# A two-block language model layer on one core: RWKV's preparation cut by one halt more, and four smaller edits in the recurrent mixers

## The reference, cut to what matters

```
rwkv:  kk = l2norm(k * k_k);  k = k * (1 + (a - 1) * k_a)
       S_t = S_{t-1} * w_t + (S_{t-1} @ -kk) (kk * a)^T + v k^T;   y_t = S_t r_t
       y = layernorm(y) + sum(r * k * r_k) * v
mlstm: qk = silu(causal_conv(qk, 4 taps));  s = (q k^T) * exp(d - m), causal
       h = (s @ v) / max(|sum(s)|, exp(-m))
gdn:   decay_ts = exp(g_t - g_s), causal;   v and k scaled with beta
```

## Time and profile before

| | us |
|---|---|
| runs | 2463.22, 2467.28, 2469.05 |
| median | 2467.28 |
| profiled execution | 2466.33 |
| its span, first to last instruction | 2464.5 |
| TensorE busy | 2414.3 |
| VectorE busy | 1414.4 |
| ScalarE busy | 1130.9 |
| GpSimd busy | 111.8 |
| mean granted TensorE clock, of full | 0.995 |

### The profile page before, as it was taken

How to read it: one execution, slowest core, us unless ns; L and a number is a source line. 1 busy time by engine, 2 the same in 40 slices (tenths; PEclk the granted TensorE clock), 3 DMA queues, 4 the chain that set the end, 5 groups by cost and what they waited for, 6 DMA issues and landing times. The chain is left out here.

```text
span 2464.5 us, 34356 instructions
## 1 busy us (share of the span) xinstructions
PE 2414.3 (98%) x14480; PEld 2053.3 (83%) x14480; DVE 1414.4 (57%) x1836; ACT 1130.9 (46%) x1412; POOL 111.8 (5%) x100
## 2 busy tenths in 40 slices
PE   7999999999999999999999999999999999999998
PEld 7987989987888888888888878898888888888887
DVE  4766656677765555555555575444446545555554
ACT  6535435553454444444344464445544455444444
POOL 2100000220000000000000050000000000000000
PEclk9999999999999999999999999999999999999999
DMA  8633434654555566555555556655545544555564
GB/s 255 206 121 99 139 108 154 215 170 172 196 184 177 187 193 198 187 188 181 194 188 187 180 190 216 205 171 171 171 154 186 173 155 153 186 191 187 192 243 146
DMA packets 225641, 441.53 MB, mean 179 GB/s; under 512 B 11890, under 2 KB 28112, under 8 KB 223056
## 3 DMA queue, kind: packets, MB, share of 16 engines
q1 hardware_dynamic: 221744, 419.80, 51.8%
q0 software_dynamic: 3744, 19.53, 2.1%
HBM read 428.81 MB, written 10.49 MB: 178 GB/s over the span
## 5 line engine op out<-in xcount | busy, mean ns | idle before, releaser
L1268 ACT CAST ringH<-raw 128x1024 fp32r<-128x1024 f32 x780 | 817.1, 1050 | 1021.2 <-PE ps L602 877.7
L1866 DVE TENSOR_TENSOR ringL<-raw,ringH 128x1024 fp32r<-128x1024 f32 x780 | 952.9, 1238 | 451.1 <-ACT ringH L1268 450.1
L600 PE MATMUL ps<-ringH,nS 128*128 128x512 f32 x1376 | 553.9, 403 | 4.3 <-DVE ringL L1866 3.1
L602 PE MATMUL ps<-ringH,nS 128*128 128x512 f32 x1376 | 539.5, 392 | 0.0
L601 PE MATMUL ps<-ringL,nS 128*128 128x512 f32 x1376 | 538.9, 392 | 0.0
L628 PE MATMUL ps<-nS,ringH 128*128 128x256 f32 x1056 | 311.7, 295 | 9.1 <-DVE ringL L1866 7.5
L600 PEld LDWEIGHTS ps<-ringH,nS 128*128 128x128 f32 x1376 | 260.1, 189 | 59.7 <-DVE ringL L1866 6.5
L602 PEld LDWEIGHTS ps<-ringH,nS 128*128 128x128 f32 x1376 | 259.6, 189 | 55.8
L601 PEld LDWEIGHTS ps<-ringL,nS 128*128 128x128 f32 x1376 | 260.2, 189 | 49.8 <-issue 0.2
L629 PE MATMUL ps<-nS,ringH 128*128 128x256 f32 x1056 | 301.3, 285 | 0.0
L630 PE MATMUL ps<-nS,ringL 128*128 128x256 f32 x1056 | 301.1, 285 | 0.0
(11 more groups left out here) (414 smaller groups left out, 2132.4 us busy)
## 6 DMA issues: line engine op xcount, KB each, us to landing
raw<-in_w_in SPq DMA_DIRECT2D x189, 1024.0 KB, 5.1
raw<-in_ffn_w_gate SPq DMA_DIRECT2D x44, 1024.0 KB, 5.2
raw<-in_ffn_w_up SPq DMA_DIRECT2D x44, 1024.0 KB, 5.2
raw<-in_ffn_w_down SPq DMA_DIRECT2D x44, 1024.0 KB, 5.1
raw<-in_w_out SPq DMA_DIRECT2D x32, 1024.0 KB, 5.1
raw<-in_w_mem_kv SPq DMA_DIRECT2D x16, 1024.0 KB, 5.1
raw<-in_w_proj_a SPq DMA_DIRECT2D x8, 1024.0 KB, 5.2
raw<-in_w_proj_m SPq DMA_DIRECT2D x8, 1024.0 KB, 5.1
```

What stands on the lines that cost most here:

```text
L600: mm(o, XH[:, ts(j)], WH, first, False)
L602: t_of[0] = mm(o, XL[:, ts(j)], WH, False, last)
L1268: e.copy(ringH[:, h % NSPL, 0:nh * cols], raw[:, u % NRAW, h0 * cols:(h0 + nh) * cols]).then_inc(*hi.tick(h))
L1866: tt2(ringL[:, h % NSPL, o], raw[:, u % NRAW, h0 * cols:(h0 + nh) * cols], ringH[:, h % NSPL, o].bitcast(F32), SUB).then_inc(*lo.tick(h))
```

## The change

1. In RWKV's preparation the halt of `6 + 2 * hh` becomes two halts of `3 + hh`. TensorE's sums of squares and all behind them move behind the first one. ScalarE gets the new halt between the small projections' sigmoids and the exponentials, VectorE between the first difference of the decay and the rest.
2. For chunk 0 the copy of `NV` to `rhs` on VectorE is gone. TensorE reads `NV`, which ScalarE wrote, and waits for that and for the last level of the inverse.
3. ScalarE's square for the variance stands one halt earlier.
4. mLSTM's convolutions begin one halt later on all engines.
5. The mLSTM score tile has 384 columns in place of 512. The quarter that the causal mask makes zero is neither computed nor stored.
6. gdn's two broadcasts are made by transposing broadcast columns of `gcol` in place of multiplying `grow` rows with a column of the identity.

```
 TensorE, bcast
-  t = m1(b[:, 256 * j:256 * j + 256], ident[:, row + h + j:row + h + j + 1].broadcast_to([128, 128]), src, j == 0)
+  for tt in range(2):
+      t = e.transpose(b[:, 256 * j + 128 * tt:256 * j + 128 * tt + 128],
+                      gcol[:, tt, o + h + j:o + h + j + 1].broadcast_to([128, 128]), ident)
...
 TensorE, rwkv
   by_token(0, V_)
+  yield 3 + hh
   sums(rw_p, rw_a, (hh, "kk"), [u3(7)[:, k, :] for k in range(2)], 2)
-  yield 6 + 2 * hh
+  yield 3 + hh
...
-  e.wait_ge(*rw_v.at(hh, "rhs", c))
+  if c:
+      e.wait_ge(*rw_v.at(hh, "rhs", c))
+  else:
+      e.wait_ge(*rw_a.at(hh, "NV", 1))
+      e.wait_ge(*rw_v.at(hh, "inv", "xt", 4, 1))
   for n in range(4):
       inst = 2 * n + tt
-      t = m1(b[p, 64 * n:64 * n + 64], XR[p, inst, :], rhs[p, inst, :], n == 0)
+      t = m1(b[p, 64 * n:64 * n + 64], XR[p, inst, :], (rhs if c else NV)[p, inst, :], n == 0)
...
 TensorE, mlstm
-  for _ in range(4):
+  for _ in range(5):
       yield
...
-  t = m1(b[:, 256 * s:256 * s + 256], K[:, h, ts(s)], Q[:, h, :], s == 0)
+  t = m1(b[:, 256 * s:256 + 128 * s], K[:, h, ts(s)], Q[:, h, 128 * s:256], s == 0)
...
 ScalarE, rwkv
   ring.free(rw_a.now(), "rw", hh, "lora", q)
+  yield
   e.wait_ge(*rw_v.at(hh, "c"))
...
-  yield
   e.wait_ge(*rw_v.at(hh, "mu"))
   act(u3(0), u3(15), ACT.Square).then_inc(*rw_a.tick(hh, "var", 0))
+  yield
   square_roots(rw_v, rw_a, (hh, "var"), col_rw)
...
 ScalarE and VectorE, mlstm
   while not L.done(f"m{q}"):
       yield
+  yield
...
 VectorE, rwkv
   tt2(Wp, c_, sg, SUB).then_inc(*rw_v.tick(hh, "wp0"))
+  yield
   e.wait_ge(*rw_a.at(hh, "lo", 1))
...
-  if c == 0:
-      e.wait_ge(*rw_a.at(hh, "NV", 1))
-      e.tensor_copy(rv, nvv).then_inc(*rw_v.tick(hh, "rhs", 0))
-  else:
+  if c:
...
 VectorE, mlstm
-  tt2(S_, S_, ps3(ring.of("ml", "KQ", h), 2), MUL).then_inc(*ml_v.tick("S", h))
+  tt2(S_, S_, ring.of("ml", "KQ", h)[:, 0:384], MUL).then_inc(*ml_v.tick("S", h))
```

More of the change, by code:

```diff
@@ L715, in mem, with bcast @@
                 yield 2
-            def bcast(mk, name, src, row):
+            def bcast(mk, name, o):
                 for h in range(0, 4, 2):
@@ L721, in bcast @@
                     for j in range(2):
-                        t = m1(b[:, 256 * j:256 * j + 256], ident[:, row + h + j:row + h + j + 1].broadcast_to([128, 128]), src,
-                               j == 0)
+                        for tt in range(2):
+                            t = e.transpose(b[:, 256 * j + 128 * tt:256 * j + 128 * tt + 128],
+                                            gcol[:, tt, o + h + j:o + h + j + 1].broadcast_to([128, 128]), ident)
                     t.then_inc(*mk.tick(*name, h))
@@ L937, in rwkv @@
                     product("RB", Bt, Rt)
-                    rhs, Z = v3(SC + 512 * 13, 8, 64), v3(SC + 512 * 14, 8, 64)
+                    NV, rhs, Z = (v3(SC + 512 * k, 8, 64) for k in (6, 13, 14))
                     Sc = [v3(SC + 512 * 17 + 128 * k, 2, 64) for k in range(4)]
@@ L1012, in mlstm @@
                 for h in range(4):
-                    S_ = v3(MU + 1024 * (h % 2), 2, T)
+                    S_ = [v2(MU + 1024 * (h % 2) + 256 * s, 256 - 128 * s) for s in range(2)]
                     b = take("ml", "MB", h)
@@ L1033, in mlstm @@
                     for s in range(2):
-                        mm(b[:, 128 * s:256], mV[:, s, ts(h)], S_[:, s, 128 * s:256], s == 0, False)
+                        mm(b[:, 128 * s:256], mV[:, s, ts(h)], S_[s][:, :], s == 0, False)
                     for s, tt in ((0, 0), (0, 1), (1, 1)):
                         for c in range(2):
-                            o = 128 * tt + 64 * c
-                            t = m1(b[half(c), 256 + tt:257 + tt], S_[:, s, o:o + 64], ones[:, 0:1], False)
+                            o = 128 * (tt - s) + 64 * c
+                            t = m1(b[half(c), 256 + tt:257 + tt], S_[s][:, o:o + 64], ones[:, 0:1], False)
                     t.then_inc(*ml_p.tick("H", h))
@@ L1066, in gdn @@
                 e.wait_ge(*gt_v.at("end"))
-                bcast(gd_p, ("gb",), grows[2], 0)
-                bcast(gd_p, ("bb",), grows[1], 32)
+                bcast(gd_p, ("gb",), 0)
+                bcast(gd_p, ("bb",), 4)
                 yield 5
@@ L1608, in mlstm @@
                 for h in range(4):
-                    S_ = v3(MU + 1024 * (h % 2), 2, T)
+                    S_ = v2(MU + 1024 * (h % 2), 384)
                     e.wait_ge(*ml_p.at("MB", h))
@@ L2367, in mlstm @@
                     for s in range(2):
-                        t = tsc(S_[:, s, :], Mb, gcol[:, s, 8 + h:9 + h], 0.0, SUB, MAX)
+                        t = tsc(S_[:, 256 * s:256 + 128 * s], Mb[:, 128 * s:256], gcol[:, s, 8 + h:9 + h], 0.0, SUB, MAX)
                     t.then_inc(*ml_v.tick("s0", h))
                     e.wait_ge(*ml_a.at("S", h))
-                    tt2(S_[:, 0, 0:128], S_[:, 0, 0:128], mask(C_SI), MUL)
-                    tt2(S_[:, 1, 128:256], S_[:, 1, 128:256], mask(C_SI), MUL).then_inc(*ml_v.tick())
+                    tt2(S_[:, 0:128], S_[:, 0:128], mask(C_SI), MUL)
+                    tt2(S_[:, 256:384], S_[:, 256:384], mask(C_SI), MUL).then_inc(*ml_v.tick())
                     own(ml_v)
                     e.wait_ge(*ml_p.at("KQ", h))
-                    tt2(S_, S_, ps3(ring.of("ml", "KQ", h), 2), MUL).then_inc(*ml_v.tick("S", h))
+                    tt2(S_, S_, ring.of("ml", "KQ", h)[:, 0:384], MUL).then_inc(*ml_v.tick("S", h))
                     ring.free(ml_v.now(), "ml", "KQ", h)
```

## The result

The changed kernel takes **2449.59 us** (four runs, 2449.44 to 2452.89), beside 2468.16 us of the kernel before on the same chip (four runs, 2463.22 to 2469.22). The ratio is 0.9932, with a 95% interval of [0.9915, 0.9949]. It is faster, by 18.6 us or 0.7% by these medians; forecast were 2454.0 and a range of 2447 to 2463. The profiled execution took 2449.46 us with a span of 2447.7, which is 16.8 less than before.

A forecast was written before the change was run, and what follows sets the result against it. TensorE, busy 98% of the span, was taken as the bound: only its instructions, idle gaps or clock could save time. Terms summed to -13.3 us, giving 2453.0; with 0.95 for the median, 2454.0, range 2447 to 2463.

The forecast's parts named there:

- m1: mLSTM's second convolution group: gap of 3.85 goes, new gap of 1.9, 0.8 at ScalarE's copy; -1.8 us with clock.
- square: ScalarE's variance square a halt earlier: gaps 0.44 and 1.29 go, and the half-clock stretch from 387.1; -3.0 us.
- first preparation: RWKV's first half of heads: gap of 1.46 goes, TensorE waits 3.6 in the memory's factor; +2.1 us net.
- broadcast: gdn's broadcast: sixteen transposes replace eight matmuls of 256 on TensorE; -1.4 us.
- second preparation: RWKV's second half of heads: casts and subtractions go on, so the gap of 1.70 at 242.80 goes; -1.7 us.
- m0: mLSTM's first convolution group, a halt later: waits of 3.84 become 0.6, at the third piece; -3.2 us.
- copy: RWKV's first chunk read in place: the wait of 1.66 before its product goes in both halves; -3.3 us.
- Rival B: Memory's reciprocal not late, VectorE's subtractions 1 us quicker, no half clock follows in RWKV; -19.5 us, 2447.8; chance 0.10.
- the prediction's sign: On TensorE's timeline, the count of half-clock stretches before 400 us is two or less.
- A: Waits only move: mLSTM's convolutions and RWKV's second half of heads bring nothing; -6.6 us, 2460.7; chance 0.23.
- C: Transposes drop the clock behind gdn's broadcast: one half-clock stretch, +1.3 us, 2455.3; chance 0.05.
- D: Slower: eight convolution pieces before RWKV's chunk chain hold up TensorE, 21.8 us instead of 7.7; +5.8, 2473; chance 0.06.

The follow-up runs named there:

- e1: Changed kernel with the one further halt of RWKV's preparation taken out again on all three engines; 2449.34 us, ratio 0.9935.
- e2: Changed kernel with mLSTM's convolutions back at their old halt; 2453.30 us, ratio 0.9949.
- e3: Changed kernel with VectorE's copy of NV to rhs for chunk 0 put back; 2456.03 us, ratio 0.9955.
- e4: Changed kernel with ScalarE's square for the variance back at its old halt; 2455.22 us, ratio 0.9962.
- e5: Changed kernel with the mLSTM score tile at 512 columns again; 2449.80 us, ratio 0.9937.
- e12: Changed kernel with both the full mLSTM score tile and gdn's broadcasts as matmuls again; 2449.55 us, ratio 0.9939.
- e6: Changed kernel with gdn's broadcasts as matmuls again; 2449.76 us, ratio 0.9936.
- e8: Changed kernel with the memory stage one halt later, as in e7, and mLSTM's second convolution one halt later still; 2443.30 us, ratio 0.9908.
- e9: Changed kernel run once more with nothing edited; 2451.47 us, ratio 0.9946.
- e7: Changed kernel with one halt more in the memory stage, ahead of its mean; 2445.15 us, ratio 0.9919.
- e10: As e7, with mLSTM's second group of convolutions three halts later; 2444.49 us, ratio 0.9914.
- e11: As e10, with VectorE's four multiplications of gdn's keys by their decay moved behind the products; 2442.96 us, ratio 0.9909.

## Why the prediction was right

**The sum without the clock.** The forecast's terms hold -1.95 us of clock (-1.3 + 1.3 in the first half, -0.65 at m1, -1.3 at the square) and -11.35 of gaps and work. Span times clock fell by 11.7 (2451.35 to 2439.63). The whole agrees better than its terms, and that is luck: the first preparation cost 1.2 less than forecast and the broadcast gained 1.4 less, and the two cancel.

| part | forecast without clock | found, and how |
|---|---|---|
| first preparation | +2.1 | +0.9 in gaps, +0.6 to +1.0 by position (e1) |
| second preparation | -1.7 | -2.0 by position (e1) |
| mLSTM, m0 and m1 | -3.2 and -1.15 | -4.0 in gaps, -4.5 by span times clock (e2) |
| copy | -3.3 | -3.3 in gaps, -2.7 (e3) |
| square | -1.7 | -1.7 in gaps, -1.7 (e4) |
| score | -1.0 | -1.1 by position, -1.1 to -1.2 by span times clock (e5, e12) |
| gdn's broadcast | -1.4 | 0 (e6) |

The gaps and positions found add up to about -11.2, beside the 11.7.

*First preparation.* The step is right (the gap in `factor`, released by VectorE's reciprocal), its size was not. TensorE got there at 118.5, as counted (118.6). VectorE was 1.4 us earlier than counted, 120.8 in place of 122.2. VectorE's timeline after:

```profile
106.46 0.68 DVE L1908 COPY AR<-ps 128x512 f32<-128x512 f32 x1
...
110.61 0.20 DVE L2170 RECIPROCAL small<-small 128x8 f32<-128x8 f32 x1 [0.28 <-ACT small L1496]
110.73 2.31 DVE L1874 TENSOR_TENSOR ringL<-raw,ringH 128x1024 fp32r<-128x1024 f32 x2
112.95 0.16 DVE L2002 TENSOR_SCALAR small<-small 128x2 f32<-128x2 f32 x1
...
118.40 2.35 DVE L1874 TENSOR_TENSOR ringL<-raw,ringH 128x1024 fp32r<-128x1024 f32 x2
120.67 0.16 DVE L2005 RECIPROCAL small<-small 128x2 f32<-128x2 f32 x1
```

The first reciprocal was 0.6 later than counted (done at 110.8, not 110.2), though the root was waited for 0.28 and not 1.3, because the drain's copy (106.46) now stood ahead of it and VectorE's scaling beside GpSimd took 1.55 us where 0.62 was counted (105.50 before, 107.06 after). Behind it the memory's mean came at 112.95 where 114.2 was counted: the two subtractions took 2.31 us where I had kept the 3.36 of the earlier trace rows, although GpSimd was no longer beside them, and the copy that I had counted there was done. The long part behind it, 5.4, and the last two subtractions, 2.3, were as counted. Both errors were carried over from rows whose surroundings the change moves. Rival B had named the first, the subtractions.

*m1.* I forecast a gap of 1.9 and 3.07 came. GpSimd's and VectorE's timelines after, to the earlier trace rows:

```profile
195.37 3.25 POOL L2746 TENSOR_TENSOR AR<-AR 128x1024 f32<-128x1024 f32 x1 [33.73 <-ACT AR L1335]
```

```profile
195.36 1.22 DVE L1874 TENSOR_TENSOR ringL<-raw,ringH 128x1024 fp32r<-128x1024 f32 x1
199.20 1.53 DVE L2348 SCALAR_TENSOR_TENSOR AR<-AR,prm 128x256 f32<-128x256 f32 x3 [2.62 <-ACT AR L1587]
200.76 0.50 DVE L2295 TENSOR_TENSOR AR<-ps,AR 64x128 f32<-64x128 f32 x2
```

The scaling took 3.25 us, not 2.17, and VectorE's subtraction now starts with it (195.36), so the first piece came 1.1 us later. The pair stands side by side in all twelve executions that have mLSTM's later halt (3.25 or 3.26 us); in e2 and in the kernel before VectorE idles there, and it is 2.17. The rest is the forecast's mechanism: the piece in front of the addition. The 0.8 behind it, at ScalarE's copy, did not appear in the changed kernel; with the piece a halt later (e8) it does, as 1.09.

*m0.* Forecast 0.6 at the third piece, measured 0.32, from a masking as forecast. So m0 gave 3.5 in gaps (3.84 less 0.32) and m1 0.8 (3.85 less 3.07).

*Broadcast.* This step of the forecast failed: -1.4 was forecast and nothing came. I costed the removed work as time won because it stood on TensorE, without asking what TensorE would be waiting for next. The 1.43 at 502.80 in the trace of before, a low half on VectorE, was outside the stretch I had listed; on it the 1.4 had to be set off.

**The clock.** Forecast: the stretch at 103.8 goes and one comes behind `factor`, the one at 206.2 half goes, 387.1 goes. Profiled: seven became four, in the repetition five; up to 400 us three became two, in the repetition three. The stretch behind the gap of 2.37 us came in three of the eight kernels that have that gap (e3, e4, e9); the one behind the gap of 3.07 in seven of nine (not in e3, and in e7 it began before the gap had ended). So 1.3 as a certainty behind `factor` was too much. The price itself holds: a stretch costs 1.1 to 1.6 where it can be read. Which stretches come in one execution is chance, so that the profiled execution had two before 400 us, as the prediction's sign wanted, is luck; the repetition had three. The other signs came: no gap before the first chunk's product, before the square's sums or at the low half near 240. Those in `factor` and before the last chunk's product are there, at 2.37 and 3.07 where 3 to 4 and about 2 were named.

Mean spans say 2463.67 (27 runs of before) and 2449.43 (nine of the changed kernel): 14.2 less, against 13.3 forecast. Of the 14.2, 11.7 is work and gaps and 2.5 clock, by span times clock. The 18.6 of the first medians is more than the change is worth on average. The time forecast, 2454.0, started from a median of three runs, 2467.28, where the median of the 27 is 2465.09.

**The rivals.** A (the waits only move, 2460.7) is out: e2 shows mLSTM's part worth 4 us, and e1 the second preparation 2.0. It holds for one edit that it did not name, the broadcast. B (more than counted, 2447.8) is out: its reason was right (the subtractions were 1 us quicker), but the reciprocal was still late by 2.37 of the 3.6, and half clock did follow. Its sum is also wrong: it takes off 1.3 for half clock at the end, twice the 0.65 that the forecast had left there (at m1), so it should say 2448.5. C (transposes drop the clock) did not show. The sixteen transposes in the timeline after, and the windows around them (of TensorE alone):

```profile
467.19 1.91 PE L723 MATMUL ps<-cm,gcol 128*128 128x128 f32 x16
```

```profile
460.00:470.00 10.00, 10.00 (x87) 1.00 0.26 83
470.00:480.00 10.00, 10.00 (x85) 1.00 0.52 166
```

The clock stays at 1.00, and e6, without them, is no different. By the Trainium skill, "TensorE: Matmul & The Clock Gate", Part 4, work in transpose mode doesn't count as busy in the same way as matmuls do. At this length (1.91 us) nothing of that shows in the clock here. What the transposes did change is the wait behind them: a stretch stands at that wait in four of the eleven executions where it is 2.47 us or more (e3, e9, e10, e11), and in none of the three where it is 1.42 to 1.44. Fourteen executions don't settle whether that is more than chance. D (eight pieces exposed over 2 us each) is out: the gaps behind pieces are 0.32 and 3.07, 3.4 in all.

One thing stays open: what decides whether a stretch comes. The one at 434.1 stands behind the 64 one-column instructions, with no gap, and so does one in five more executions (448.5 in the kernel before, and in e3, e5, e6 and e9); in the other eight the clock stays full behind the same instructions. No run was made on it.

## What to carry to other kernels

Cut work on the busiest engine only counts as far as the next thing it waits for is early enough; look for the next gap behind the edit, even 20 us on, before booking it. A duration taken from a row holds for that row's company: when a halt is moved, ask what GpSimd and VectorE then do at the same time, and take the row without company for the one and with it for the other. To size edits of 1 to 3 us under a clock whose drops differ between executions, undo them one by one and compare the distance between two instructions around the edit that have no half-clock stretch between them, or span times clock, rather than medians.

## What the runs showed of the hardware

- The same program, with gaps that differ by at most 0.03 us, had four half-clock stretches in one execution and five in another, partly at other places. A stretch of 3.4 us cost 1.1 to 1.6 us, by the distance of the same two instructions with and without it (14.14 and 13.07, 52.94 and 51.39). The spans of 27 runs of the kernel before lie within 9 us, and span times clock is the same to 0.3 us in three series.
- GpSimd's multiplication of 128x1024 took 2.17 us alone and 3.25 or 3.26 with a VectorE subtraction started beside it, in twelve executions of twelve; two such subtractions took 2.31 without GpSimd and 3.36 with it. VectorE's two scalings of 128x256 took 0.62 us without GpSimd (at 105.50 before) and 1.55 beside it (at 107.06 after).
- A gap of 0.8 us was followed by a half-clock stretch (304.4), and so was a group of 64 one-column matmul instructions with no gap at all (434.1, and in six executions of fourteen); a gap of 2.37 us was followed by one in three executions of eight.
